# Sample attention of a hybrid decoder trunk: two batches in one softmax tile, and value products by head pair in 32-column groups

## The chip, the cores and the metric

The kernel runs on one core of a Trainium2 chip. The metric is the time of one execution on the device in microseconds (us). The core has a matrix engine (TensorE, PE in the rows; its weight loads are PEld), VectorE (DVE), ScalarE (ACT), GpSimd (POOL), SyncE (SP), which here only issues DMAs, and 16 DMA engines. PE multiplies a stationary operand of up to 128x128 with a moving one; a product with 32 stationary columns uses one of four groups of 32 columns of the array and writes the 32 partitions of PSUM that belong to it.

## The reference

Two decoder layers over one prompt of 512 tokens and 8 sample batches of 8 new tokens. Each layer has three mixers (GLA, HGRN2 and softmax attention), an output projection and a channel mixer. The change is in the softmax attention of the sample batches. It has 8 heads of 64 dims, and each new token sees 1024 cached keys and the new ones at three dilations:

```python
def dilated_attention_sample(q, k, v, kbuf, vbuf):
    kc = jnp.concatenate([kbuf.astype(k.dtype), k], axis=1)
    vc = jnp.concatenate([vbuf.astype(v.dtype), v], axis=1)
    parts = []
    for window, dil in DILATED_GROUPS:       # ((128, 1), (512, 4), (2048, 16))
        band = window // dil
        idx = buf + jnp.arange(T)[:, None] - dil * jnp.arange(band + 1)[None, :]
        valid = idx >= 0
        kg = kc[:, idx]
        vg = vc[:, idx]
        s = jnp.einsum('bthd,btkhd->bthk', q, kg).astype(jnp.float32) * scale
        s = jnp.where(valid[None, :, None, :], s, -jnp.inf)
        m = jnp.max(s, axis=-1)
        p = jnp.exp(s - m[..., None])
        parts.append((m, jnp.sum(p, axis=-1), jnp.einsum('bthk,btkhd->bthd', p, vg.astype(jnp.float32))))
    return combine_dilations(parts), kc[:, T:], vc[:, T:]
```

The kernel computes all three dilations as one softmax over all 1024 + 64 keys, with the logarithm of how often a key occurs in the three groups added to its score (`smask` for the cache, `smask_new` for the new keys, where those of other batches are masked away).

## The kernel before

Every engine has its own program, written by hand, and they meet on semaphores. A layer runs through the input projections, the linear mixers, the prompt attention, the sample attention, the output projection (L882 among others) and the channel mixer.

The sample attention (PE program L1082 to L1123) loops over 8 batches `b`. Its state:

- `Qs` holds, for each batch and head pair `hp` (0 to 3), a 128x32 stationary operand: two heads of 64 dims in rows, 8 tokens of the first head in columns 0 to 7, 8 of the second in 8 to 15. The other 16 columns are zero. VectorE writes it in L1499 and L1503, just ahead of the prompt attention.
- The scores of a batch stand in PSUM banks 0 to 2. Head pair `hp` has partitions 32hp to 32hp+31, of which 16 are live. The products are L1105 (1024 cached keys, in two of 512) and L1106 (64 new keys).
- VectorE scales and masks them into a softmax tile `Ps` in L1543 and L1545 and takes the maximum in L1548; ScalarE takes the exponential and its sum in L790; VectorE takes the reciprocal in L1557. PE transposes the tile (L1092, L1093), and ScalarE copies it out of PSUM (L785, L786) into `PTs`.
- Values: for each of 8 chunks of 128 keys, one product with the transposed tile as stationary operand (128 columns, all head pairs) and all 512 value columns as moving one (L1118), and one over the new keys (L1120). Each 32-row group thus also gets the columns of the three other head pairs, which nobody reads.
- VectorE takes the 128 columns of each head pair and scales them into `Os` (L1534, four instructions of 32 rows). PE turns `Os` (L1096), and VectorE copies both halves into `mix` (L1553, L1554), the input of the output projection.

PE runs in an interleaved order: in step `b` it transposes the tile of batch b-1, turns the output of b-2, makes the scores of b and the values of b-1.

The cache of keys and values comes in pieces of 1 MB, four a batch (keys in two pieces by head pairs, L481; values in two halves of four chunks, L484). There are 7 buffers. `piece_order` sets the order, SP issues the DMAs in it, and from the eighth piece on it first waits until PE has used the piece that had the buffer: `ssc_done` (after a batch's scores) for keys, `spv_half` and `spv_done` (after each half of a batch's values) for values. The first 7 are issued before the prompt attention.

All products of this stage are float32. The trace shows each as two passes, with a weight load each.

## Time and profile before

| | |
|---|---|
| median of 3 runs | 2908.32 us (2907.53 to 2909.29) |
| profiled execution, its span | 2910.4 us |
| PE busy | 2689.7 us, 92% |
| VectorE busy | 940.2 us, 32% |
| ScalarE busy | 637.7 us, 22% |
| GpSimd busy | 229.2 us, 8% |
| DMA | 360.60 MB, mean 124 GB/s |

The profile is of one execution, 2.1 us above the median. "Busy" is the share of time in which an instruction of the engine is recorded; passes of PE that run over each other are counted once. PEclk is the clock granted to TensorE, where 1.00 is 2.4 GHz and 0.50 is 1.2 GHz. A row of a timeline gives start, length, engine, line, operation, tiles and count, and in brackets how long the engine had sat idle and for whom. A row of a window gives its bounds and length, then busy time and count of instructions of PE, PEld, VectorE, ScalarE and GpSimd, the granted clock, the busy share of the 16 DMA engines and their GB/s. A count of passes is twice that of float32 products.

### The profile page before, as it was taken

The page shows a single profiled execution, that of the slowest core. Times are in us where ns is not written, and L with a number is a line of the kernel's source. Part 1 is how long each engine was busy: PE and PEld are TensorE (multiplying, and loading weights), DVE is VectorE, ACT ScalarE, POOL GpSimd, SP SyncE. Part 2 cuts the span into 40 slices and gives each one's busy share as a digit, 9 for nine tenths or more (in the row PEclk, how much of TensorE's full clock was granted, in tenths as well). Part 3 has the DMA queues.
Part 4 walks back from the last instruction along what each step waited for, and adds up shares of the span by engine and source line. Part 5 has one row for each costly group of instructions (what it writes and reads, how often), then busy time and mean ns, then how long its engine had stood idle before and what let it go on. Part 6 is the DMA issues. An engine that isn't in the chain of part 4 may idle for free. (4 is left out here: it accounts for less than half of the span.)

```text
span 2910.4 us, 36713 instructions
## 1 busy us (share of the span) xinstructions
PE 2689.7 (92%) x14894; PEld 2134.0 (73%) x14894; DVE 940.2 (32%) x1787; ACT 637.7 (22%) x1092; POOL 229.2 (8%) x328
## 2 busy tenths in 40 slices
PE   7996878999799999999888889998999999999998
PEld 5993444535599999979744444467899999999996
DVE  3237454322223223133465443312022222222122
ACT  3453222211222122133622232101010000000000
POOL 2003331000100000020042210000000000000000
PEclk9997565599899999999866656997799999999997
DMA  4531003073364464235200032701454644555461
GB/s 159 184 130 48 0 1 117 1 260 116 129 225 152 150 230 147 64 121 182 102 4 1 2 116 85 277 15 42 127 179 138 213 161 162 171 180 159 137 213 57
DMA packets 79894, 360.60 MB, mean 124 GB/s; under 512 B 9296, under 2 KB 9696, under 8 KB 70816
## 3 DMA queue, kind: packets, MB, share of 16 engines
q1 hardware_dynamic: 76640, 350.85, 35.5%
q0 software_dynamic: 3136, 8.06, 0.8%
q8 instruction: 88, 1.44, 0.2%
q14 instruction: 30, 0.25, 0.0%
HBM read 350.03 MB, written 75.43 MB: 146 GB/s over the span
## 5 line engine op out<-in xcount | busy, mean ns | idle before, releaser
L1258 PE MATMUL ps<-scratch,weight_ring 128*128 128x160 f32 x2816 | 398.9, 300 | 1.5 <-ACT scratch L839 1.4
L1258 PEld LDWEIGHTS ps<-scratch,weight_ring 128*128 128x128 f32 x2816 | 388.8, 191 | 2.3 <-ACT scratch L839 1.9
L888 PE MATMUL ps<-ffn_in_hi,weights_hi 128*128 128x288 f32 x704 | 210.5, 299 | 23.3 <-DVE weights_lo L1578 22.1
L1733 DVE TENSOR_TENSOR scratch<-scratch,ps 128x160 f32<-128x160 f32 x88 | 28.2, 321 | 609.2 <-ACT scratch L855 609.2
L1263 PE MATMUL ps<-scratch,weight_ring 128*128 128x160 f32 x1408 | 211.0, 304 | 0.0
L888 PE MATMUL ps<-ffn_in_lo,weights_hi 128*128 128x288 f32 x704 | 209.3, 297 | 0.0
L888 PE MATMUL ps<-ffn_in_hi,weights_lo 128*128 128x288 f32 x704 | 208.5, 296 | 0.0
L1263 PEld LDWEIGHTS ps<-scratch,weight_ring 128*128 128x128 f32 x1408 | 193.8, 190 | 10.5 <-issue 10.5
L888 PE MATMUL ps<-proj_in_hi,proj_weights_hi 128*128 128x288 f32 x608 | 182.6, 300 | 0.0
L855 ACT ACTIVATE scratch<-ps 128x160 f32<-128x160 f32 x88 | 26.8, 304 | 708.7 <-PE ps L1258 708.7
L888 PE MATMUL ps<-proj_in_lo,proj_weights_hi 128*128 128x288 f32 x608 | 179.3, 295 | 0.0
L888 PE MATMUL ps<-proj_in_hi,proj_weights_lo 128*128 128x288 f32 x608 | 178.7, 294 | 0.0
L888 PEld LDWEIGHTS ps<-ffn_in_hi,weights_hi 128*128 128x128 f32 x704 | 133.5, 190 | 24.2 <-issue 24.2
L1210 PE MATMUL ps<-scratch,values 128*128 128x160 f32 (+1 forms) x720 | 137.8, 339 | 4.3 <-DVE scratch L1673 4.3
L888 PEld LDWEIGHTS ps<-ffn_in_hi,weights_lo 128*128 128x128 f32 x704 | 134.2, 191 | 0.0
L888 PEld LDWEIGHTS ps<-ffn_in_lo,weights_hi 128*128 128x128 f32 x704 | 133.9, 190 | 0.0
L1210 PEld LDWEIGHTS ps<-scratch,values 128*128 128x128 f32 (+1 forms) x720 | 111.1, 204 | 30.0 <-issue 30.0
L882 PE MATMUL ps<-normed_or_mixed,weight_ring 128*128 128x288 f32 x512 | 128.1, 414 | 1.1 <-DVE normed_or_mixed L1554 1.1
L731 ACT ACTIVATE scratch<-scratch 128x448 f32<-128x448 f32 (+22 forms) x198 | 75.2, 390 | 213.8 <-POOL scratch L574 96.5
L882 PEld LDWEIGHTS ps<-normed_or_mixed,weight_ring 128*128 128x128 f32 x512 | 99.2, 194 | 29.4 <-DVE normed_or_mixed L1554 1.5
L1578 DVE TENSOR_TENSOR weights_lo<-weight_ring,weights_hi 128x1024 fp32r<-128x1024 f32 (+1 forms) x60 | 80.2, 1343 | 119.2 <-ACT weights_hi L806 119.2
L994 PE MATMUL ps<-scratch,constants 128*64 128x512 f32 x192 | 106.6, 674 | 10.6 <-DVE scratch L1439 7.8
(298 smaller groups left out, 4505.7 us busy)
## 6 DMA issues: line engine op xcount, KB each, us to landing
weight_ring<-w_gu SPq DMA_DIRECT2D x220, 512.0 KB, 4.2
weight_ring<-w_dn_moe SPq DMA_DIRECT2D x88, 512.0 KB, 3.6
ok_s<-kcache SPq DMA_DIRECT2D x16, 2032.0 KB, 10.2
ov_s<-vcache SPq DMA_DIRECT2D x16, 2032.0 KB, 9.9
scratch<-kcache SPq DMA_DIRECT2D x20, 1024.0 KB, 7.3
scratch<-vcache SPq DMA_DIRECT2D x20, 1024.0 KB, 5.7
weight_ring<-w_feat SPq DMA_DIRECT2D x38, 512.0 KB, 3.7
linear<-vcache SPq DMA_DIRECT2D x12, 1024.0 KB, 6.5
```

What stands on the lines that cost most here:

```text
L731: nc.scalar.activation(v, v, ACT.Exp).then_inc(exp_ready, 1)
L855: nc.scalar.activation(tg[:, f % 2, :], ps[:, 3 + f % 2, 0:CAP], ACT.Silu).then_inc(silu_ready, 1)
L882: op = nc.tensor.matmul(out_pair[:, a, :], w, rhs[:, a * HALF:a * HALF + HALF], start=k == 0, stop=k == kn - 1)
L888: op = nc.tensor.matmul(out, x, y, start=k == 0 and n == 0, stop=k == kn - 1 and n == 2)
L994: nc.tensor.matmul(ps[0:64, 0, :], const["to_row"][:, o:o + 64], Pr[:, j % 2, 0:SEQ], start=j == 0, stop=j == BLK - 1).then_inc(prod_used, 1)
L1210: op = nc.tensor.matmul(out, H_tok[0:rows, tt, k * P:k * P + P], Sel[0:rows, tt, :], start=tt == 0, stop=tt == TT)
L1258: op = nc.tensor.matmul(ps[:, 3 + f % 2, o:o + CAP], w[:, k, :], Xg[:, k, :], start=k == 0, stop=k == KC - 1)
L1263: op = nc.tensor.matmul(ps[:, k // 3, (k % 3) * CAP:(k % 3) * CAP + CAP], w[:, k, :], hidg[:, f, :], start=f == 0 and k % 3 == 0, stop=f = ...
L1578: v.tensor_tensor(Wl[:, j % NSPLIT, 0:w], ring[:, n % R, 0:w], Wh[:, j % NSPLIT, 0:w], ALU.subtract).then_inc(w_split, 1)
L1733: v.tensor_tensor(hidg[:, f, :], tg[:, f % 2, :], ps[:, 3 + f % 2, CAP:2 * CAP], ALU.mult).then_inc(hid_ready, 1)
```

## The change

Two batches share one softmax tile. The 32 stationary columns of a head pair now hold 16 of the even batch (`i` = 0) and 16 of the odd (`i` = 1); for each batch the other half of the columns is zero. The scores of both are accumulated in the same PSUM rows. The loop runs over 4 pairs `u`, so mask, maximum, exponential, transposes, copies and the turn of the output come once per pair. In the scores the head pairs are now the inner loop, ahead of the two halves of keys.

The value product of a chunk is four products per batch, one per head pair: 32 stationary columns, and as moving operand the head pair's own 128 value columns. The two batches accumulate in banks 6 and 7, each for all 32 rows of a head pair. VectorE takes the right rows of both by multiplying with two columns (`rden_pair`), the reciprocal sum in the rows of one batch and zero in the others. Both are added into `Os`. The query copies become 16 instead of 8. `piece_order` now has the keys of a pair ahead of the values of the pair before.

```diff
-CONSTS = [("ones", P), ("lnc", SEQ), ("smask", PAST), ("smask_new", NB * NS), ("cos", T), ("sin", T), ("mask16", P),
+NPAIR = NB // 2
+CONSTS = [("ones", P), ("lnc", SEQ), ("smask", PAST), ("smask_new", NPAIR * NS), ("pair_rows", 2), ("cos", T), ("sin", T), ("mask16", P),
...
     row = p % 32
     t = row % DEC
-    live = row < 2 * DEC
     d = PAST + t - np.arange(PAST)[None, :]
-    c["smask"] = np.where(live, log_mult(d, d >= 0), 0).astype(np.float32)
+    c["smask"] = log_mult(d, d >= 0)
...
+        new.append(log_mult(d, (d >= 0) & (key // DEC == 2 * pair + row // (2 * DEC))))
+    c["pair_rows"] = (row // (2 * DEC) == np.arange(2)[None]).astype(np.float32)
...
-        piece_order = [(b - (part >= 2), part) for b in range(NB + 1) for part in range(4)
-                       if 0 <= b - (part >= 2) < NB]
+        piece_order = [(2 * (u - lag) + b, 2 * lag + half) for u in range(NPAIR + 1) for lag in range(2) if 0 <= u - lag < NPAIR
+                       for b in range(2) for half in range(2)]
...
-                for b in range(NB + 2):
-                    q = (b - 1) % 2
-                    if 1 <= b <= NB:
-                        n = NB * L + b - 1
+                for u in range(NPAIR + 2):
+                    q = (u - 1) % 2
+                    if 1 <= u <= NPAIR:
+                        n = NPAIR * L + u - 1
                         pe.wait_ge(sp_ready, n + 1)
-                        if b >= 2:
+                        if u >= 2:
                             pe.wait_ge(spt_ready, n)
                         for c in range(8):
                             nc.tensor.transpose(ps[:, 3 + c // 4, (c % 4) * P:(c % 4) * P + P], Ps[:, q, c:PAST:8], const["ident"])
                         nc.tensor.transpose(ps[0:NS, 5, 0:P], Ps[:, q, PAST:PAST + NS], const["ident"]).then_inc(spt_ps, 1)
-                    if b >= 2:
-                        pe.wait_ge(os_ready, NB * L + b - 1)
-                        nc.tensor.transpose(ps[:, 6 + b % 2, 0:P], Os, const["ident"]).then_inc(os_turned, 1)
-                    if b < NB:
-                        n = NB * L + b
-                        kc = [tiles(piece_landed(pe, L, b, part), 2) for part in range(2)]
-                        if b:
-                            pe.wait_ge(ssc_free, n)
-                        for hp in range(4):
-                            o = slice(32 * hp, 32 * hp + 32)
+                    if u >= 2:
+                        pe.wait_ge(os_ready, NPAIR * L + u - 1)
+                        nc.tensor.transpose(ps[:, 6, P:2 * P], Os, const["ident"]).then_inc(os_turned, 1)
+                    if u < NPAIR:
+                        if u:
+                            pe.wait_ge(ssc_free, NPAIR * L + u)
+                        for i in range(2):
+                            b = 2 * u + i
+                            kc = [tiles(piece_landed(pe, L, b, part), 2) for part in range(2)]
                             for a in range(2):
-                                nc.tensor.matmul(ps[o, a, :], Qs[:, b, hp, :], kc[hp // 2][:, hp % 2, a * 512:a * 512 + 512], start=True, stop=True)
-                            op = nc.tensor.matmul(ps[o, 2, 0:NS], Qs[:, b, hp, :], QK[:, 4 + hp, SEQ:T], start=True, stop=True)
-                        op.then_inc(ssc_done, 1)
-                    if 1 <= b <= NB:
-                        n = NB * L + b - 1
+                                for hp in range(4):
+                                    nc.tensor.matmul(ps[32 * hp:32 * hp + 32, a, :], Qs[:, b, hp, :], kc[hp // 2][:, hp % 2, a * 512:a * 512 + 512],
+                                                     start=i == 0, stop=i == 1)
+                            for hp in range(4):
+                                op = nc.tensor.matmul(ps[32 * hp:32 * hp + 32, 2, 0:NS], Qs[:, b, hp, :], QK[:, 4 + hp, SEQ:T],
+                                                      start=i == 0, stop=i == 1)
+                            op.then_inc(ssc_done, 1)
+                    if 1 <= u <= NPAIR:
+                        n = NPAIR * L + u - 1
                         pe.wait_ge(spt_ready, n + 1)
-                        if b >= 3:
-                            pe.wait_ge(smix_ready, n - 1)
-                        pt, out = tiles(PTs[:, q, :], 9), ps[:, 6 + q, :]
-                        for half in range(2):
-                            vc = tiles(piece_landed(pe, L, b - 1, 2 + half), 4)
-                            for c in range(4):
-                                op = nc.tensor.matmul(out, pt[:, 4 * half + c, :], vc[:, c, :], start=(half, c) == (0, 0), stop=False)
-                            if half:
-                                op = nc.tensor.matmul(out, pt[0:NS, 8, :], V[0:NS, TT, 512:1024], start=False, stop=True)
-                            op.then_inc((spv_half, spv_done)[half], 1)
-                pe.wait_ge(smix_ready, NB * (L + 1))
+                        if u >= 2:
+                            pe.wait_ge(smix_ready, n)
+                        pt = tiles(PTs[:, q, :], 9)
+                        for i in range(2):
+                            b = 2 * (u - 1) + i
+                            for half in range(2):
+                                vc = tiles(piece_landed(pe, L, b, 2 + half), 4)
+                                for c in range(4):
+                                    for hp in range(4):
+                                        o = slice(32 * hp, 32 * hp + 32)
+                                        op = nc.tensor.matmul(ps[o, 6 + i, 0:P], pt[:, 4 * half + c, o], vc[:, c, hp * P:hp * P + P],
+                                                              start=(half, c) == (0, 0), stop=False)
+                                if half:
+                                    for hp in range(4):
+                                        o = slice(32 * hp, 32 * hp + 32)
+                                        op = nc.tensor.matmul(ps[o, 6 + i, 0:P], pt[0:NS, 8, o], V[0:NS, TT, 512 + hp * P:512 + hp * P + P],
+                                                              start=False, stop=True)
+                                op.then_inc((spv_half, spv_done)[half], 1)
+                pe.wait_ge(smix_ready, NPAIR * (L + 1))
...
-                        op = v.tensor_copy(Qs[r, :, hp, hb * DEC:hb * DEC + DEC], QK[r, hp, SEQ:T].rearrange("p (b t) -> p b t", b=NB))
+                        for i in range(2):
+                            o = (2 * i + hb) * DEC
+                            op = v.tensor_copy(Qs[r, i:NB:2, hp, o:o + DEC], QK[r, hp, SEQ:T].rearrange("p (b t) -> p b t", b=NB)[:, i:NB:2])
...
-                for b in range(NB + 2):
-                    if b >= 2:
-                        dve.wait_ge(spv_done, NB * L + b - 1)
-                        if b >= 3:
-                            dve.wait_ge(os_turned, NB * L + b - 2)
-                        for hp in range(4):
-                            r = slice(32 * hp, 32 * hp + 32)
-                            op = v.tensor_scalar(Os[r], ps[r, 6 + b % 2, hp * P:hp * P + P], rden[r, 4 + b % 2:5 + b % 2], None, ALU.mult)
-                        op.then_inc(os_ready, 1)
-                        dve.wait_ge(os_ready, NB * L + b - 1)
-                    if b < NB:
-                        n = NB * L + b
-                        pn, s = Ps[:, b % 2, :], 4 + b % 2
-                        dve.wait_ge(ssc_done, n + 1)
-                        if b >= 2:
+                for u in range(NPAIR + 2):
+                    pair_col = rden_pair[:, 2 * (u % 2):2 * (u % 2) + 2]
+                    if u >= 2:
+                        dve.wait_ge(spv_done, NB * L + 2 * (u - 1))
+                        link(v.tensor_scalar(Os, ps[:, 6, 0:P], pair_col[:, 0:1], None, ALU.mult))
+                        v.scalar_tensor_tensor(Os, ps[:, 7, 0:P], pair_col[:, 1:2], Os, ALU.mult, ALU.add).then_inc(os_ready, 1)
+                        dve.wait_ge(os_turned, NPAIR * L + u - 1)
+                        o = ps[:, 6, P:2 * P].rearrange("p (h i x) -> p h i x", h=4, i=2)
+                        t = SEQ + 2 * DEC * (u - 2)
+                        for hb in range(2):
+                            r = slice(hb * DH, hb * DH + DH)
+                            op = v.tensor_copy(mix[r, 4:8, t:t + 2 * DEC].rearrange("p h (i x) -> p h i x", i=2), o[r, :, :, hb * DEC:hb * DEC + DEC])
+                        op.then_inc(smix_ready, 1)
+                    if u < NPAIR:
+                        n = NPAIR * L + u
+                        pn, s = Ps[:, u % 2, :], 4 + u % 2
+                        dve.wait_ge(ssc_done, NB * L + 2 * (u + 1))
+                        if u >= 2:
                             dve.wait_ge(spt_ps, n - 1)
                         v.scalar_tensor_tensor(pn[:, 0:PAST], ps[:, 0:2, :].rearrange("p a t -> p (a t)"), DH ** -0.5,
                                                const["smask"], ALU.mult, ALU.add)
                         v.scalar_tensor_tensor(pn[:, PAST:PAST + NS], ps[:, 2, 0:NS], DH ** -0.5,
-                                               const["smask_new"][:, b * NS:b * NS + NS], ALU.mult, ALU.add).then_inc(ssc_free, 1)
+                                               const["smask_new"][:, u * NS:u * NS + NS], ALU.mult, ALU.add).then_inc(ssc_free, 1)
                         dve.wait_ge(ssc_free, n + 1)
                         v.tensor_reduce(negmax[:, s:s + 1], pn, AX.X, ALU.max, negate=True).then_inc(smx_ready, 1)
-                    if b >= 2:
-                        dve.wait_ge(os_turned, NB * L + b - 1)
-                        o = ps[:, 6 + b % 2, 0:P].rearrange("p (h q) -> p h q", h=4)
-                        t = SEQ + DEC * (b - 2)
-                        v.tensor_copy(mix[0:DH, 4:8, t:t + DEC], o[0:DH, :, 0:DEC])
-                        v.tensor_copy(mix[DH:P, 4:8, t:t + DEC], o[DH:P, :, DEC:2 * DEC]).then_inc(smix_ready, 1)
-                    if b < NB:
+                    if u < NPAIR:
                         dve.wait_ge(sp_ready, n + 1)
                         link(v.reciprocal(rden[:, s:s + 1], den[:, s:s + 1]))
+                        link(v.tensor_scalar(pair_col, const["pair_rows"], rden[:, s:s + 1], None, ALU.mult))
```

ScalarE's loop changes in the same manner, from `b` and `NB` to `u` and `NPAIR`, with the same instructions.

PE, a middle step of the loop, before. L1092 and L1093 are transposes, L1096 the turn of the output, L1105 and L1106 the scores, L1118 and L1120 the values; `linear` and `scratch` are the memories that hold buffers and tiles:

```order
L1092 MATMUL ps<-constants,scratch 128x128 x8
L1093 MATMUL ps<-constants,scratch 64x128
L1096 MATMUL ps<-constants,linear 128x128
L1105 MATMUL ps<-linear 32x512 x2
L1106 MATMUL ps<-attn_qk,linear 32x64
...
L1118 MATMUL ps<-scratch 128x512 x8
L1120 MATMUL ps<-values,scratch 128x512
```

PE, the same place now, one step for a pair (L1107 and L1110 are the scores, L1126 and L1131 the values):

```order
L1094 MATMUL ps<-constants,scratch 128x128 x8
L1095 MATMUL ps<-constants,scratch 64x128
L1098 MATMUL ps<-constants,linear 128x128
L1107 MATMUL ps<-linear 32x512 x8
L1110 MATMUL ps<-attn_qk,linear 32x64 x4
L1107 MATMUL ps<-scratch,linear 32x512 x8
L1110 MATMUL ps<-attn_qk,linear 32x64 x4
L1126 MATMUL ps<-scratch 32x128 x32
L1131 MATMUL ps<-values,scratch 32x128 x4
L1126 MATMUL ps<-linear,scratch 32x128 x32
L1131 MATMUL ps<-values,scratch 32x128 x4
```

The eight products 512 wide have become 32 products 128 wide for each batch, the scores of four head pairs follow each other, and one set of transposes serves two batches.

VectorE, a middle step before (L1534 scales the output, L1543 to L1548 prepare the softmax, L1553 and L1554 copy to `mix`):

```order
L1534 TENSOR_SCALAR linear<-ps,small 32x128 x4
L1543 SCALAR_TENSOR_TENSOR scratch<-ps,constants 128x1024
L1545 SCALAR_TENSOR_TENSOR scratch<-ps,constants 128x64
L1548 TENSOR_REDUCE small<-scratch 128x1
L1553 COPY normed_or_mixed<-ps 64x4x8
L1554 COPY normed_or_mixed<-ps 64x4x8
L1557 RECIPROCAL small<-small 128x1
```

VectorE, the output part of a step now, at the end of a layer's sample attention:

```order
L1545 TENSOR_SCALAR linear<-ps,small 128x128
L1546 SCALAR_TENSOR_TENSOR linear<-ps,small,linear 128x128
L1552 COPY normed_or_mixed<-ps 64x4x16 x2
```

Four instructions of 32 rows have become two of 128 rows, and the copies to `mix` come right behind the output's turn, ahead of the next pair's softmax.

SP, the pieces of the cache at the start of a layer's sample attention, before:

```order
L481 DMA scratch<-kcache 128x2048 x4
L484 DMA linear<-vcache 128x2048 x2
L481 DMA linear<-kcache 128x2048
L481 DMA scratch<-kcache 128x2048
L484 DMA scratch<-vcache 128x2048 x2
```

And now:

```order
L483 DMA scratch<-kcache 128x2048 x4
L483 DMA linear<-kcache 128x2048 x3
L483 DMA scratch<-kcache 128x2048
L486 DMA scratch<-vcache 128x2048 x3
L486 DMA linear<-vcache 128x2048
```

Eight pieces of keys now lead, then the four of values of the first pair.

## Rows read from the trace of the kernel before

**Rows 1.** The page: span, and busy time of each engine

```profile
span 2910.4 us, 36713 instructions
PE 2689.7 (92%) x14894; PEld 2134.0 (73%) x14894; DVE 940.2 (32%) x1787; ACT 637.7 (22%) x1092; POOL 229.2 (8%) x328
```

**Rows 2.** Busy time by window: both stages, and one steady batch

```profile
579.30:704.70 125.40, 115.91 (x417) 47.45 (x417) 36.03 (x80) 19.78 (x32) 0.00 (x0) 0.99 0.56 210
1790.80:1916.20 125.40, 115.88 (x417) 47.41 (x417) 36.03 (x80) 19.79 (x32) 0.00 (x0) 0.99 0.56 209
605.57:620.21 14.64, 14.26 (x53) 5.91 (x53) 4.48 (x10) 2.45 (x5) 0.00 (x0) 1.00 0.78 289
```

**Rows 3.** Timeline of PE, one batch

```profile
617.24 1.12 PE L1120 MATMUL ps<-values,scratch 64*128 64x512 f32 x2
618.29 1.17 PE L1092 MATMUL ps<-constants,scratch 128*128 128x128 f32 x8
...
619.95 0.33 PE L1096 MATMUL ps<-constants,linear 128*128 128x128 f32 x1 [0.38 <-DVE linear L1534]
620.21 1.93 PE L1105 MATMUL ps<-scratch,linear 128*32 128x512 f32 x6
...
624.82 7.13 PE L1118 MATMUL ps<-linear,scratch 128*128 128x512 f32 x16
```

**Rows 4.** State update in 32-column groups: timeline, all instructions of the line, window

```profile
291.21 1.08 PE L1017 MATMUL ps<-values,scratch 128*32 128x64 f32 x32 [0.51 <-DVE scratch L1469]
...
L1017 PE MATMUL ps<-values,scratch x128: 313/314/369, 291.2 to 1656.4; 128*32 128x64 f32 x64, 128*64 128x64 f32 x64
...
291.20:292.30 1.10, 1.09 (x34) 0.92 (x36) 0.00 (x0) 0.00 (x0) 0.00 (x0) 0.50 0.00 0
```

**Rows 5.** Timeline: the first softmax of layer 0

```profile
584.04 1.23 DVE L1543 SCALAR_TENSOR_TENSOR scratch<-ps,constants 128x1024 f32<-128x1024 f32 x1 [10.61 <-PE ps L1106]
...
585.43 1.28 DVE L1548 TENSOR_REDUCE small<-scratch 128x1 f32<-128x1088 f32 x1
586.75 1.20 ACT L790 ACTIVATE scratch<-scratch,small 128x1088 f32<-128x1088 f32 x1 [7.50 <-DVE small L1548]
...
588.10 1.25 PE L1092 MATMUL ps<-constants,scratch 128*128 128x128 f32 x8 [4.09 <-ACT scratch L790]
```

**Rows 6.** DMA in the stage of layer 0, and windows of it

```profile
q1 hardware_dynamic: 3600, 26.22, 56.2%
...
584.00:585.00 1.00, 0.00 (x1) 0.00 (x0) 0.96 (x1) 0.00 (x0) 0.00 (x0) 1.00 0.17 33
...
586.00:587.00 1.00, 0.00 (x0) 0.00 (x0) 0.71 (x1) 0.25 (x1) 0.00 (x0) 1.00 0.87 344
587.00:591.00 4.00, 2.90 (x11) 1.38 (x12) 0.16 (x1) 2.22 (x4) 0.00 (x0) 0.75 0.92 387
599.00:605.00 6.00, 5.91 (x20) 2.63 (x18) 1.30 (x5) 0.76 (x3) 0.00 (x0) 1.00 1.03 414
...
629.00:633.00 4.00, 4.00 (x10) 1.31 (x8) 0.16 (x1) 0.00 (x0) 0.00 (x0) 1.00 1.01 426
```

**Rows 7.** Granted clock by window (PEclk): prompt attention, after a wait, output projection

```profile
440.00:579.00 139.00, 127.07 (x398) 70.57 (x396) 55.19 (x153) 38.47 (x107) 12.46 (x20) 0.50 0.16 62
...
588.10:592.40 4.30, 4.30 (x15) 1.74 (x17) 0.14 (x1) 1.18 (x2) 0.00 (x0) 0.61 0.59 248
...
704.70:708.50 3.80, 3.80 (x9) 2.75 (x10) 0.00 (x0) 0.00 (x0) 0.00 (x0) 0.55 0.00 0
708.50:712.30 3.80, 3.80 (x17) 2.96 (x17) 0.00 (x0) 0.00 (x0) 0.00 (x0) 1.00 0.01 4
```

**Rows 8.** Timeline: the end of layer 0's sample attention

```profile
702.28 1.43 DVE L1534 TENSOR_SCALAR linear<-ps,small 32x128 f32<-32x128 f32 x4 [8.28 <-PE ps L1120]
```

**Rows 9.** Timeline: query copies and the first step of the prompt attention

```profile
470.10 1.21 DVE L1503 COPY linear<-attn_qk 64x64 f32<-64x64 f32 x8
...
471.69 1.64 PE L1059 MATMUL ps<-attn_qk 64*128 64x384 f32 x2 [0.94 <-DVE scratch L1514]
```

More of the change, by code:

```diff
@@ L268, in build @@
         rden = SM[:, 56:64]
+        rden_pair = SM[:, 0:4]
         ebl = tiles(SM[:, 64:64 + CT * 12], CT)
@@ new lines, in _ @@
+                    if 1 <= u <= NPAIR:
+                        n = NPAIR * L + u - 1
+                        pe.wait_ge(spt_ready, n + 1)
+                        if u >= 2:
[16 more added lines that the diff above has]
+                                op.then_inc((spv_half, spv_done)[half], 1)
```

18 lines of the change are left out of this document (8 added, 10 removed).

## The prediction

> **What bounds the kernel now.** I read the page first: one core, span 2910.4 us, TensorE busy 92%, VectorE 32% [rows 1]. Such an average does not say what the edited stage is worth, so the second view is busy time by window. The sample attention runs once in each layer, 579.3 to 704.7 and 1790.8 to 1916.2 us: twice 125.4 us, with PE busy 115.9 of them and DMA at a share of 0.56 [rows 2]. A window of one steady batch lasts 14.64 us, PE busy 14.26 in it; VectorE has 4.5 us of work, ScalarE 2.5 [rows 2]. So eight batches in a row are bound by PE, and the next resource is the DMA (0.78 of its time), not the softmax.
>
> The third view is PE's order in time. A float32 product appears in the trace as two passes. In a batch the value products take 7.13 us for their 16 passes of 512 columns, 0.45 us each, and the one over the new keys 1.12 more; from the first transpose to the turn of the output pass 1.66 us, 0.38 of it a wait, so the transposes take 1.3, and the turn 0.33 [rows 3]. What is left of the batch, from 620.21 to 624.82, is 4.6 us of scores [rows 3]. Summed serially, 16 score passes at 0.45 us would be 7.2 us: passes of different 32-column groups already run over each other, though the order (all of one head pair, then the next) lets only neighbours do so.
>
> **PE's part of the change.** The value product of a chunk is now four products of 128 columns, each in its own 32-column group, instead of one of 512. Per batch that is 36 products, 72 passes, for 9 products, 18 passes. The cost hangs on whether four groups run together. The state update shows exactly this pattern, four heads in four 32-column groups, one after another: 32 passes end 1.08 us after the first begins, 34 ns apiece, where one pass alone is recorded with at least 313 ns, at a granted clock of 0.50 (1.2 GHz) [rows 4]. Four passes together are 135 ns for 64 columns at half clock, so 135 ns for 128 columns at full clock if the rate follows the clock. From the other side, a 512-column pass of 0.45 us gives 0.11 us for 128 columns. 18 sets a batch are therefore 2.0 to 2.4 us; I take 2.2, against 8.2 now.
>
> The scores get head pairs innermost, so four groups follow each other directly: 4 passes of 0.45 plus two short ones, 1.9 us a batch. The other bound is no more overlap than now, 4.6 us. I take 1.9, nearest to the update's row; no row shows four groups at full clock, so 4.6 stays in the range. Transposes (1.3), the output turn (0.33) and their waits come once per pair.
>
> At full clock PE then needs for a pair of batches 3.8 (scores) + 4.4 (values) + 1.3 + 0.3 + about 0.5 of waits = 10.3 us, 15.7 with the scores' upper bound. Before, it was 2 x 14.64 = 29.3.
>
> **The softmax chain.** From VectorE's start to the first transpose, 584.04 to 588.10, pass 4.1 us: 1.23 and 1.28 on VectorE and 1.20 on ScalarE are most of it [rows 5]. With PE's step ahead of it I count 4.2. The tiles keep their size but serve two batches; rows that were dead are used, and time goes by columns. So the chain occurs four times a layer instead of eight, and beside it lie the value products of the previous pair (4.4 us). Only the first is exposed, as before; the DMA bound below covers it. PE waits twice more for an output to be copied out, both once per pair, behind transposes.
>
> **What becomes late: the cache.** None of this changes the bytes. 25 pieces of 1 MB are loaded inside a stage (7 sit there when it starts), 26.22 MB on the hardware queue [rows 6]. Where the queue is full, the lowest and the highest of five windows of 4 to 6 us show 414 and 426 GB/s, at shares of 1.03 and 1.01 [rows 6]. At 420 GB/s a piece is 2.5 us, a pair of batches (8 pieces) 20.0 us. That is nearly double PE's 10.3: the stage turns from PE-bound to DMA-bound, and most of PE's gain is lost. With 7 buffers, a DMA needs only the buffer seven pieces back. In pair rhythm PE's longest stretch without a release (transposes, turn, first scores) is about 4 us, less than two pieces' time, so the queue should stay full once it is.
>
> The stage per layer by steps:
> - first batch's scores until its buffers come free: 1.9 us;
> - issue to flowing data: 1.5 us (33 GB/s in the first microsecond, 344 in the third [rows 6]);
> - a gap while PE waits for the first softmax and then scores batch 2. PE is back at 3.8 + 4.2 + 1.3 = 9.3 us, ends batch 2 at about 11 to 12.5 (the clock has been 0.5 after this wait [rows 7]), and four pieces have been queued until then: they land until 3.4 + 10 = 13.4. The next data flow at 12.5 to 14. I take 0.7;
> - 26.22 MB at 420 GB/s: 62.4 us;
> - the last half batch of values, 10 sets of passes, 1.1 us at full clock to 2.7 at half: 1.6;
> - the tail. Now 2.4 us, from 702.28 to the stage's end at 704.7, of it 1.43 for four copies of 32 rows [rows 2, 8]; afterwards two of 128 rows at 0.35 each: 1.9 with the wait ahead.
>
> Sum 70.0 us, against 125.4: 55.4 saved.
>
> **What it costs elsewhere.** The query copies on VectorE are 16 instead of 8, each half as long. 8 take 1.21 us, and VectorE's first step of the prompt attention comes behind them, for which PE then waits 0.94 us [rows 9]. Between 0 and 1.2 us are added; 0.8 taken. A stage in which PE waits half the time may hand a low clock to the output projection: there 3.80 us at 0.55 did 9 passes, and the next 3.80 at 1.00 did 17 [rows 7], so each 3.8 us more at half clock costs 1.8. Part of this is paid already; 1.0 taken, 0 to 2. The constants shrink by 254 columns, at nothing: they load at the start, behind other work. Two layers: 2 x (55.4 - 1.8) = 107.2; 2910.4 - 107.2 = 2803.2 us. The median of the runs, 2908.32, is 2.1 below the profiled span, so I forecast **2801 us**.
>
> **The clock.** The rows show PE at 0.61 right after a 4 us wait, and at 0.50 through the whole prompt attention though PE was called busy 127 of 139 us [rows 7]. So in a stage that waits for data 1.2 GHz is possible throughout. Then values are 8.8, scores 7.6, transposes and turn 3.4: 19.8 us a pair by my upper value price, about 18 by the lower, still at or under 20.0.
>
> The Trainium skill (TensorE: Matmul & The Clock Gate, "HAM oscillation") says that a loop whose compute bursts are shorter than its DMA waits is put back to half clock in each burst. By that rule this stage runs at 1.2 GHz, which makes the first rival below the outcome; the rows just named agree that it falls after a wait, and none shows a DMA-paced stage.
>
> **Rivals.** (1) *Turns instead of cover.* At 1.2 GHz PE has no slack, and the 3.4 us at the head of each pair, in which no buffer is released, add to the 20.0 instead of lying beside them: 4 x 3.4 x 2 = 27 us, 2828 us. For it: the clock rows. Against: seven buffers. (2) *A slower stream.* No row shows more than some 8 us of full queue without a pause; the new stage asks for over 60. At 387 GB/s, a window in which the queue filled [rows 6], it is 67.8 us instead of 62.4: 2812 us. (3) *Slower than before.* The small products don't overlap: 72 passes a batch at 0.11 us are 7.9, scores in series 7.2 a batch, a pair 15.8 + 14.4 + 2.1 = 32.3 us against 29.3, so 12 us a layer: 24 more than 2908, 2932 us. It decides from 29.3 us a pair, that is once both products lose nearly all overlap. Against it stand the rows of the update, and the scores of today that already overlap.
>
> **How the numbers follow.** DMA-bound with little lost, 2790 to 2812: 0.71. Rival 2, 2812 to 2822: 0.08. Rival 1 or a part of it, 2822 to 2840: 0.13. Rival 3: 0.04. The rest, 0.04, lies between 2840 and 2900. The low end is 426 GB/s (1.8 us less), no cost for copies and clock (3.6), no gap (1.4) and a last half batch at full clock (1.0): 2793, rounded down. Range 2790 to 2840, which leaves out less than 1 in 10 by these cases; I keep it there since no case ends between. Measurement tells 0.2% (6 us) from no change. Faster 0.95, same 0.01, slower 0.04.
>
> **What would show each step.** In the profile after: the stage near 70 us in both layers; DMA share near 1.0 and about 400 GB/s over it; PE busy clearly under its length if the clock is high; value passes starting four together, about 27 to 34 ns apiece. PE's waits should be for pieces that land, not for VectorE or ScalarE. Wrong if DMA pauses at each pair's head (rival 1), if its share is full at fewer GB/s (rival 2), or if value passes start 0.1 us apart (rival 3). The output projection's first 4 us tell the clock term.

## The result

The changed kernel takes 2805.94 us, median of 4 runs (2803.39 to 2809.07), against 2908.81 of the kernel before (4 runs): a ratio of 0.9647, interval 0.9633 to 0.9661. The forecast was 2801. A second series of 5 runs gave 2808.24, ratio 0.9655 (0.9641 to 0.9669). The profiled execution lasted 2803.6 us; the sum of the prediction was 2803.2.

The page after, which answers to [rows 1]:

```profile
span 2803.6 us, 38139 instructions
PE 2544.7 (91%) x15678; PEld 2087.7 (74%) x15678; DVE 902.4 (32%) x1715; ACT 617.5 (22%) x1060; POOL 230.5 (8%) x328
```

PE is still called busy 91% of the span. What happened is seen by window only: first both stages, then four stretches of them (us, busy time and instructions of PE, PEld, DVE, ACT and POOL, granted clock, DMA share, GB/s). They answer to [rows 2] and [rows 6].

```profile
575.90:648.10 72.20, 47.02 (x809) 27.44 (x809) 16.71 (x36) 9.89 (x16) 0.00 (x0) 0.91 0.90 365
1732.00:1808.00 76.00, 48.49 (x815) 27.72 (x813) 16.71 (x36) 10.49 (x17) 0.00 (x0) 0.88 0.86 346
592.00:600.00 8.00, 4.47 (x109) 3.20 (x98) 2.93 (x8) 2.47 (x4) 0.00 (x0) 1.00 1.01 423
600.00:610.00 10.00, 6.75 (x88) 2.74 (x91) 1.27 (x2) 0.00 (x0) 0.00 (x0) 0.83 1.01 424
630.00:640.00 10.00, 6.26 (x158) 4.62 (x159) 2.74 (x7) 2.47 (x4) 0.00 (x0) 1.00 1.02 420
1760.00:1770.00 10.00, 8.75 (x84) 3.32 (x88) 1.06 (x1) 0.00 (x0) 0.00 (x0) 0.55 1.01 424
```

From the first score product to the output projection it is now 72.1 us in layer 0 (575.94 to 648.08) and 74.6 in layer 1 (1733.35 to 1807.99), against 125.3 twice. PE works 47 of 72 us. In the four short windows DMA stands at a share of 1.01 or 1.02 and 420 to 424 GB/s, both where PE was busy 56% and where it was busy 88%, mostly at half clock (0.55). This looks as if the bound had moved to the cache's transfer; the first experiment tests it.

PE's timeline shows what became cheap (start, duration, engine, line, tile, count, in brackets the wait ahead and what ended it); it answers to [rows 3] and [rows 5]:

```profile
575.94 1.92 PE L1107 MATMUL ps<-scratch,linear 128*32 128x512 f32 x16 [0.73 <-issue]
583.92 1.59 PE L1094 MATMUL ps<-constants,scratch 128*128 128x128 f32 x8 [4.12 <-ACT scratch L792]
590.43 1.92 PE L1126 MATMUL ps<-scratch 128*32 128x128 f32 x64
592.28 0.42 PE L1131 MATMUL ps<-values,scratch 64*32 64x128 f32 x8
592.63 1.08 PE L1126 MATMUL ps<-scratch 128*32 128x128 f32 x32
599.98 1.92 PE L1107 MATMUL ps<-linear 128*32 128x512 f32 x16 [2.94 <-DMA linear<-kcache]
604.97 3.59 PE L1107 MATMUL ps<-scratch,linear 128*32 128x512 f32 x16 [2.95 <-DMA scratch<-kcache]
625.00 3.27 PE L1107 MATMUL ps<-scratch,linear 128*32 128x512 f32 x16 [2.93 <-DMA scratch<-kcache]
642.44 1.08 PE L1126 MATMUL ps<-scratch 128*32 128x128 f32 x32 [1.06 <-DMA scratch<-vcache]
644.90 1.08 PE L1126 MATMUL ps<-scratch 128*32 128x128 f32 x32 [1.38 <-DMA scratch<-vcache]
647.20 0.33 PE L1098 MATMUL ps<-constants,linear 128*128 128x128 f32 x1 [0.86 <-DVE linear L1546]
```

A batch's values are 64 passes in 1.92 us, 30 ns apiece, and with the new keys 2.2 us from 590.43 to 592.63. From 594.30 on most stretches of scores or values start behind a piece that lands.

The trace's DMA records give each piece's landing. Each piece leaves 16 records, one for each DMA engine's part, and counts when the last is there. The records do not name the engine: "first engine" stands for a piece's earliest record, "slowest" for its latest. Worked out from them, in us (the third column is for the last piece):

```
                 queue's   stream of the   landing of   last landing   from there to
                 start     first engine:   slowest      from stage's   the output
                 latency   gaps in it      behind first start          projection
layer 0          1.8       0.98            1.95         68.92          3.22
layer 1          1.8       1.24            4.03         71.27          3.37
```

The first column is the time from SP's first issue, 2.1 us into the stage, to the first engine's first landing, less a piece's 2.485 us. Twenty-five pieces at 2.485 us (422 GB/s) are 62.1. In layer 0 that is 2.1 + 1.8 + 62.1 + 0.98 + 1.95 = 68.9.

### The profile page after: what moved, and what is told of

Read it like the earlier page. It is cut to its first block, busy times and chain, and to the rows that moved or that the text cites. A ratio compares the mean times of both kernels' runs of the same rounds, so it can differ in the third digit from the quotient of the medians.

```text
span 2803.6 us, 38139 instructions
## 1 busy us (share of the span) xinstructions
PE 2544.7 (91%) x15678; PEld 2087.7 (74%) x15678; DVE 902.4 (32%) x1715; ACT 617.5 (22%) x1060; POOL 230.5 (8%) x328
## 4 chain that ended last, share of the span: by engine, by line
PE 84%; DVE 6%; DMA 4%; ACT 3%; issue 2%; POOL 1%; SPq 0%; DVEq 0%; ACTq 0%; POOLq 0%
PE ps L890 24%; PE ps L1270 14%; PE ps L1275 7%; PE ps L884 7%; PE ps L1222 5%; PE ps L1244 4%; PE ps L931 4%; PE ps L1061 3%; PE ps L1080 2%; DMA scratch<-kcache 2%; PE ps L996 2%; PE ps L988 2%; PE ps L1069 1%; PE ps L1035 1%; DVE scratch L1451 1%
```

## The experiments

Two theories stood against each other for most of them. *DMA*: the stage is paced by the landings, and PE and the softmax lie under them. *PE or softmax*: a remaining wait between engines paces it. A second question was which of the change's parts brings the gain: the values by groups, the head pairs innermost in the scores, or the pairing. "Stage" is as above, layer 0 and layer 1 of the profiled execution.

### Half the bytes

```diff
+                            w = 1 if at < NPC else 2
-                                sp.dma_start(tiles(pieces[slot], 2), d["kcache"][L, b][:, 2 * part:2 * part + 2]).then_inc(piece_in[slot], 16)
+                                sp.dma_start(tiles(pieces[slot], 2)[:, :, 0:1024 // w], d["kcache"][L, b][:, 2 * part:2 * part + 2, 0:1024 // w]).then_inc(piece_in[slot], 16)
```

`w` is 2 from the eighth piece on, so half of the cache is left out. The values' pieces are halved in the same way.

> The changed kernel, but from the eighth piece of a layer on only half of each cache piece is loaded (half of the keys' columns, two of four value chunks); the products run over all columns as before, on old data. So half of the cache is left out, and the work of every engine is unchanged. My theory (the stage is paced by the DMA): the data take 31 us instead of 62, PE becomes the bound with about 10.3 us a pair, and the stage falls from 72 to 74 us to 47 to 52 us in each layer. Rival (turns instead of cover, PE at 1.2 GHz with some 19 us a pair): the stage stays near 65 to 70 us. Rival (PE or the softmax chain paces the stage already): it stays at 72 or more.

The stages took 52.0 and 50.5 us, 20.1 and 24.2 less. The total, 2862.4 us in one run, can't be compared: the stage's wrong values go on to the later parts, and PE does 16366 passes instead of 15678. In the stage nothing was left out but bytes:

```profile
592.00:612.00 20.00, 17.01 (x332) 10.84 (x332) 6.84 (x16) 4.95 (x8) 0.00 (x0) 1.00 1.02 380
```

The *DMA* theory holds: with the same instructions on PE, VectorE and ScalarE the stage shrinks by 20 us or more. It doesn't show a stage that is free of the DMA, though. PE fills 85% of these 20 us, and the DMA share is still 1.02, at 380 GB/s: halving a piece also changed its packets, 4752 for 13.11 MB in layer 0 where the changed kernel has 3600 for 26.22. The stage came out in the upper part of the expected 47 to 52 us.

### The groups one after another

```diff
-                                for c in range(4):
-                                    for hp in range(4):
+                                for hp in range(4):
+                                    for c in range(4):
```

> The changed kernel, with the head pairs as the outer loop of the value products: the 16 passes of one 32-column group (8 at a time, per half batch) come before those of the next, with the same products. Theory (what makes 72 passes a batch cheap is that four groups run together, which needs neighbours in the order): the passes of one group follow each other at 0.107 us, and only neighbours at the seams overlap, as in the old scores. A batch's values then take 4 to 7.5 us instead of 1.9 to 2.2, a pair of batches 14 to 21 us of PE. Below 20 us the DMA still hides it and the stage stays at 72 to 76 us; above, it grows by 4 times the excess, at most to 85. Rival (the array keeps all four groups busy whatever the order): value passes still start 27 ns apart.

Ratio 0.9662 (0.9644 to 0.9680), stages 76.0 and 77.1 us, about at the upper end of what was expected. PE's timeline, one batch at full clock:

```profile
612.89 4.34 PE L1126 MATMUL ps<-scratch 128*32 128x128 f32 x64
617.16 0.42 PE L1131 MATMUL ps<-values,scratch 64*32 64x128 f32 x8
```

The same 64 passes take 4.34 us instead of 1.92 when eight passes, four products, in a row go to the same group. That more than doubles the price of the values. In layer 0's stage PE is busy 62.8 us instead of 47.0, and yet the stage is only 3.8 us longer (2.5 in layer 1), and the ratios, 0.9662 and 0.9655 for the changed kernel, are not told apart; their intervals are too wide to show these 6 us. In layer 0 the last piece lands 69.4 us after the start (68.9 without the edit), and most of the extra appears behind it, 6.5 us to the projection instead of 3.2, where nothing covers PE's work. In layer 1 it lands at 72.2 (71.3), and the projection starts 5.0 us later (3.4). The overlap of four groups is real, but inside the stage most of it isn't needed.

### Pairs with wide values

The tiles of pairs stay; L1126 and L1131 become one product of 128x512 and one of 64x512 per chunk again, and VectorE scales in eight steps of 32 rows.

> The changed kernel with the pair tile, but each batch's value products as before: 128 stationary columns and 512 value columns for each chunk, and VectorE takes the blocks it needs (eight instructions of 32 rows). It has the pairing and the new score order, without the 32-column groups for values. PE needs 3.8 + 16.4 + 1.6 + 0.5 = 22.3 us a pair, over the DMA's 20.0. Theory: stage 4 x 22.3 plus about 8 for the first scores, the first softmax and the end = 97 us, 28 below the kernel before, about 2853 us in all. If pairing were worthless, it would be 104 or more (the score order alone).

Ratio 0.9829 (0.9806 to 0.9853), stages 104.9 and 105.0: slower than expected by 8 us, and inside the range that the expectation gave for pairing that is worth nothing. The timeline shows one reason:

```profile
609.86 1.12 PE L1126 MATMUL ps<-values,scratch 64*128 64x512 f32 x2
610.91 1.16 PE L1094 MATMUL ps<-constants,scratch 128*128 128x128 f32 x8
611.91 0.27 PE L1095 MATMUL ps<-constants,scratch 128*64 128x128 f32 x1
614.04 0.33 PE L1098 MATMUL ps<-constants,linear 128*128 128x128 f32 x1 [1.86 <-DVE linear L1545]
```

The eight scalings stand between the last value product and the turn, and PE waits about 1.86 us for them in each pair (3.00 behind the last). A pair takes 23.4 us (614.04 to 637.47), bound by PE. Pairing and the order of the scores together bring 48 us in the medians (2910.6 to 2862.4) without the groups, under half of the gain. How little of it is the pairing's shows below, where the order stands alone.

### Groups for the values, no pairs

```diff
-                                op = nc.tensor.matmul(out, pt[:, 4 * half + c, :], vc[:, c, :], start=(half, c) == (0, 0), stop=False)
+                                for hp in range(4):
+                                    o = slice(32 * hp, 32 * hp + 32)
+                                    op = nc.tensor.matmul(out[o, 0:P], pt[:, 4 * half + c, o], vc[:, c, hp * P:hp * P + P], start=(half, c) == (0, 0), stop=False)
...
-                        for hp in range(4):
-                            r = slice(32 * hp, 32 * hp + 32)
-                            op = v.tensor_scalar(Os[r], ps[r, 6 + b % 2, hp * P:hp * P + P], rden[r, 4 + b % 2:5 + b % 2], None, ALU.mult)
+                        v.tensor_scalar(Os, ps[:, 6 + b % 2, 0:P], rden[:, 4 + b % 2:5 + b % 2], None, ALU.mult).then_inc(os_ready, 1)
```

The base is the kernel before; scores and softmax remain per batch.

> The kernel before, one batch per tile and its old score order, with only the value products by head pair in 32-column groups, and one scaling instruction of 128 rows instead of four. PE per batch: 4.6 scores + 2.0 values + 1.6 transposes and turn = 8.2 us, plus what shows of the softmax chain: 4.2 us from the last score to the next transposes, of which the values cover only 2.0, so about 2 us more, and 0.4 of wait for the turn. 10.8 us a batch against 10.0 of the DMA. Theory: stage 8 x 10.8 + 6 = 92 us, 33 below the kernel before, about 2842 us. If the softmax chain is hidden, the stage is DMA-bound at 84 to 87 as 8 x 10 plus ends.

Ratio 0.9730 (0.9714 to 0.9746), median 2831.2; stages 89.2 and 89.1, 3 us under the expected 92. Two rows of PE's timeline, a batch apart, and a window:

```profile
605.49 1.16 PE L1092 MATMUL ps<-constants,scratch 128*128 128x128 f32 x8 [2.05 <-ACT scratch L790]
...
615.63 1.16 PE L1092 MATMUL ps<-constants,scratch 128*128 128x128 f32 x8 [2.05 <-ACT scratch L790]
```

```profile
605.00:625.00 20.00, 16.18 (x212) 9.06 (x212) 6.88 (x14) 4.67 (x9) 0.00 (x0) 1.00 0.99 391
```

A batch is 10.14 us, 2.05 of it a wait for the exponential. The DMA moves 391 GB/s, close to the 422 of the changed kernel but not there.

### The order of the scores alone

Base is the kernel before; the head pairs become the inner loop in the scores, the values stay 512 wide.

> The kernel before with one edit: in the scores the head pairs are innermost, so four 32-column groups follow each other. One batch per tile, value products 512 columns wide. Scores fall from 4.6 to 1.9 us a batch; nothing waits newly, since the 8.2 us of value products cover the softmax. Theory: a batch takes 14.64 - 2.7 = 11.9 us, the stage 8 x 2.7 = 21 to 22 us less than 125.3, that is 104 us, about 2864 to 2868 us in all. Since the run with the pair tile and wide values had 105 us, pairing without narrow values would then have been worth nothing. Rival (pairing is worth what it saves on transposes): this stage is 110 us or more.

Ratio 0.9850 (0.9835 to 0.9865), stages 105.0 and 104.2.

```profile
606.96 0.62 PE L1105 MATMUL ps<-scratch,linear 128*32 128x512 f32 x2
606.97 0.62 PE L1105 MATMUL ps<-linear 128*32 128x512 f32 x2
...
608.70 0.29 PE L1108 MATMUL ps<-attn_qk,linear 128*32 128x64 f32 x8
608.93 6.28 PE L1120 MATMUL ps<-linear,scratch 128*128 128x512 f32 x14
```

The scores of a batch last 2.0 us, 606.96 to the first value pass at 608.93, instead of 4.6 [rows 3]: 2.6 us for each of 8 batches, 21 a stage. The stage is 1 us over the expected 104 or on it, the median, 2863.6, just under the expected range. With pairs on top, two sections above, the stage was the same 105 us: as long as the values stay wide, pairing brought nothing. Two batches take 24.0 us here and 23.4 as a pair, and that is lost again at the end: in layer 0 two batches of values instead of one stand behind the last softmax, and a wait of 3.00 us for the scalings instead of 1.52.

### Both orders, no pairs

The two edits above together.

> The kernel before with one batch per softmax tile, but both of PE's regroupings: value products by head pair in 32-column groups, and head pairs innermost in the scores. Per batch PE does 1.9 + 2.2 + 1.6 us and waits about 2 to 2.5 for the softmax, whose 4.2 us are covered only by the values: 7.7 to 8.2 us a batch, under the DMA's 10.0. Theory (the DMA is the bound and pairing only makes PE's share smaller below it): stage 71 to 76 us, like the changed kernel, some 2800 to 2812 us in all. Rival (pairing is what brings the stage below 89 us): 85 us or more, 2825 and up.

Ratio 0.9653 (0.9636 to 0.9669), median 2808.10: the same as the changed kernel's 2808.24 beside it. In steady state the DMA is full too:

```profile
605.00:625.00 20.00, 13.18 (x224) 7.73 (x216) 6.88 (x14) 5.08 (x9) 0.00 (x0) 0.93 1.01 422
```

The stages are 77.6 and 77.4, above the expected range. SP's issues and the landings say why. Timeline of SP:

```profile
580.34 0.33 SPq L481 DMA_DIRECT2D scratch<-kcache  x1
580.72 8.92 SPq L484 DMA_DIRECT2D scratch<-vcache  x2
589.68 0.43 SPq L481 DMA_DIRECT2D scratch<-kcache  x1
```

Before the first softmax only one batch's keys can be released, so two pieces are queued (580.34, 580.72), and the queue then runs dry: 4.4 us of gap in the first engine's stream. Pairs release four pieces there, and the gap is 1.0. This is the larger part of what pairing does for the stage, 5 us per layer in the profile: 3.4 and 3.3 us are the gap, 1.1 and 0.9 a slowest engine that is further behind (3.05 and 3.25 us against 1.98 and 2.32), 0.8 and 0.6 the way from the last landing to the projection. In the total it isn't seen. In this profile the parts around the stage, which the edit doesn't touch, were shorter by 5.1 us in all than in the changed kernel's beside it (span 2806.0 less 155.0 against 2800.8 less 144.7); whether that is chance or has a cause is left open.

### The scores of the second pair first

In the changed kernel the first softmax leaves PE idle for 4.12 us. Here the scores of pair 1 are issued ahead of the transposes of pair 0, in that wait.

`scores()` is the block of score products, unchanged, put in a function.

```diff
+                    if u == 1:
+                        scores()
                     if 1 <= u <= NPAIR:
...
+                    if u != 1:
+                        scores()
```

> The changed kernel with one move on PE: the scores of the second pair come ahead of the transposes of the first, so they fill the 4 us in which PE waits for the first softmax, and the buffers of the second pair's keys come free some 5 us earlier. Theory (the stage lost time in the gap before the twelfth piece, whose buffer waits for batch 2's scores): the landings stay 2.48 us apart from the first to the last, no gap of 3.5 or 4.5 us between the fourth and fifth, the last piece lands 1 to 3 us earlier after the stage's start, stage 69 to 72 us, 2 to 6 us less in all than the changed kernel. Rival (the gap is start-up latency of the queue or one lagging DMA engine, whatever the order): the landings keep their gap and nothing moves.

> The changed kernel itself, as a reference for the next two on the same chip. Expected 0.9647 of the kernel before, as measured (0.9633 to 0.9661), stages of 72 to 75 us.

Ratio 0.9637 (0.9618 to 0.9655) beside 0.9655 (0.9641 to 0.9669) for the changed kernel: the intervals overlap. Stages 71.1 and 72.1 against 72.2 and 72.5. The landings separate two things. The gap in the first engine's stream fell from 1.03 to 0.08 us in layer 0 and from 1.05 to 0.77 in layer 1. The slowest engine's delay did not: 1.98 and 2.32 us before, 1.73 and 2.26 now. So the theory was half right: in layer 0 PE's late release makes the gap of one microsecond. In layer 1 it makes about half of it: 0.5 of the 1.05 us stood between the fourth and the sixth landing and is gone, and 0.5 stood between the first and the second, where no release is late; that time is 3.00 us without the edit and 3.21 with it. The three later traces with this order have 0.0 to 0.3 us of gap in both layers.

### Work for PE's waits

PE waits 18 us of layer 0's stage and 20 of layer 1's for the DMA. The first four of the output projection's eight k-steps read only what the linear mixers left, and so need nothing of the sample attention. In this kernel, on top of the last edit, the first four k-steps of its units 0 and 1 are issued between the last value pieces.

```diff
+EARLY_OUT = {(3, 0, 1): 0, (4, 0, 0): 1}
...
+                                m = EARLY_OUT.get((u, i, half))
+                                if m is not None:
+                                    pe.wait_ge(ssc_free, NPAIR * (L + 1))
+                                    w = landed(ring_n + m)[:, 0:1024].rearrange("p (k c) -> p k c", k=KC)
+                                    for k in range(4):
+                                        gemm(pair(m), w[:, k, :], mix[:, k, :], k, KC)
...
-                    for k in range(KC):
+                    for k in range(4 if m in EARLY_OUT.values() else 0, KC):
```

> The kernel of the run before last (second pair's scores first), and in PE's waits for the last cache pieces the first half (four of eight steps, the ones that read the linear mixers' outputs) of the first two units of the output projection: 32 passes, 7.7 us of work for each layer, moved from behind the stage into it. Theory (PE is idle for 5 us or more of each 10 us there, and only the DMA paces the stage): the stage does not get longer by more than 1 us, the projection behind it is 7.7 us shorter, 13 to 16 us less in all than the run before last. Rival (PE at 1.2 GHz has no time to give): the stage grows by as much as the projection shrinks, and the gain is under 5 us.

> The kernel with the early first halves of two units of the output projection, again, as the reference of the run before it on the same chip: 0.9587 of the kernel before (0.9572 to 0.9602), stage 74 us in both layers.

2789.29 us, ratio 0.9587 (0.9572 to 0.9602), and again 2787.74, 0.9586 (0.9573 to 0.9599). It is 14 us below the kernel of the last section, as expected, and 0.7% below the changed kernel. PE's timeline at the end of layer 0's stage:

```profile
629.66 4.15 PE L885 MATMUL ps<-normed_or_mixed,weight_ring 128*128 128x288 f32 x16
...
639.52 4.15 PE L885 MATMUL ps<-normed_or_mixed,weight_ring 128*128 128x288 f32 x16
643.60 1.08 PE L1132 MATMUL ps<-scratch 128*32 128x128 f32 x32
644.61 0.42 PE L1137 MATMUL ps<-values,scratch 64*32 64x128 f32 x8
644.96 1.95 PE L1132 MATMUL ps<-scratch 128*32 128x128 f32 x64
```

8.3 us of projection were moved, and the stage grew from 71.1 to 73.8: 5.6 us hidden; in layer 1, 72.1 to 73.8, it is 6.6. That the stage would grow by no more than 1 us was wrong. The last 64 value passes have no wait ahead of them, since the last piece had landed at 643.2. More than that: from 629.66 on PE doesn't wait for a piece any more (its only wait up to the last values is 1.16 us for ScalarE, ahead of 638.51). PE has become the bound of the last 20 us.

### More of it

The last four k-steps over the first 288 tokens, which are all prompt tokens, are moved too, for both units: 4.4 us more.

> As the early projection, with more of it: of the first two units also the last four steps over the first 288 tokens, which are all prompt tokens, so 24 of 32 passes of each unit, 5.8 us twice in each layer, now stand in PE's waits for the last eight value pieces. PE is idle there some 11 us. Theory: the stage grows by 1 to 2 us against the early projection (73.8), the projection behind it shrinks by 3.9, a gain of 3 to 6 us in all. Rival (PE's slack there is used up, since each value piece already waits for a lump of 4 us): the stage grows by 3.9 or more and nothing is gained.

2785.93 us, ratio 0.9583 (0.9569 to 0.9597), not to be told from the 2787.74 beside it, so the expected gain isn't there. The trace agrees:

```profile
646.36 2.21 PE L1146 MATMUL ps<-normed_or_mixed,weight_ring 128*128 128x288 f32 x8
648.50 1.96 PE L1132 MATMUL ps<-scratch 128*32 128x128 f32 x64
```

The last piece lands at 642.3, 68.1 us after the start as before the edit. One of the two added lumps stands behind it (646.36), the other ahead of it (633.88), but in the stretch in which PE had no wait for a piece left. So neither is hidden: the stage is 78.3 us, less 12.7 moved is 65.6; before, 73.8 less 8.3 is 65.5.

## Why the prediction was right

- **What it turns on.** That the stage changes from PE-bound to DMA-bound was shown by halving the bytes and, from the other side, by doubling the price of the values: 15.8 us more of PE's work lengthened layer 0's stage by 3.8.
- **Value products**, 2.2 us a batch taken: 2.20 measured. Scores 1.9 taken: 16 passes in 1.92 at full clock. The state update's passes at half clock [rows 4] were the right row, and the rate follows the clock (34 ns for 64 columns there, 30 for 128 here).
- **26.22 MB**, 62.4 us taken: 62.1, at 422 GB/s over more than 60 us. Rival 2 (a slower stream in the long run) is out. The Trainium skill (DMA: Bandwidth & Descriptors, Bandwidth) gives 425 GB/s for a 16 MB load by a core that streams alone. The trace agrees with its 422; with the 79.0 us that the same row gives for those 16 MB, half that rate, it does not.
- **Head and tail.** First scores 2.1 (1.9 taken), start of the queue 1.8 (1.5), from the last landing to the projection 3.2 and 3.4 (1.6 + 1.9).
- **The gap** is the term that was mis-sized: 0.7 taken. It is 1.0 and 1.2 in the stream itself, and a second part wasn't in the sum at all, 2.0 and 4.0 us by which the slowest of the 16 engines lags behind the first. Together 2.9 and 5.3. So the stages are 72.1 and 74.6 instead of 70.0. Nor is all of the gap where the prediction put it, behind the first softmax: in layer 0 it is, in layer 1 0.8 of its 1.24 us stand between the first three landings.
- **Copies.** 0.8 taken; PE now waits 1.59 for the prompt attention's first step, 0.94 before [rows 9]: 0.65.

```profile
466.83 1.87 DVE L1517 COPY linear<-attn_qk 64x32 f32<-64x32 f32 x16
469.07 1.65 PE L1061 MATMUL ps<-attn_qk 64*128 64x384 f32 x2 [1.59 <-DVE scratch L1528]
```

- **The clock behind the stage.** 1.0 taken a layer. Windows of the output projection after, as [rows 7]:

```profile
648.10:651.90 3.80, 3.80 (x16) 3.02 (x17) 0.00 (x0) 0.00 (x0) 0.00 (x0) 1.00 0.00 0
1808.00:1811.80 3.80, 3.80 (x8) 2.80 (x9) 0.00 (x0) 0.00 (x0) 0.00 (x0) 0.50 0.02 4
```

In layer 0 it starts at full clock, where before it started at 0.55: 7 more passes, about 1.6 us gained. In layer 1 it starts at 0.50, and in the first 7.6 us it does 22 passes, 26 before: 0.9 us lost. Over both the term came out at no cost, where 2.0 us were priced.

- **The total.** The stages gave back 53.2 and 50.7 us, 103.8 instead of 110.8. The total still came out near, as the rest of the kernel, priced at a cost of 3.6 us, became 3.0 shorter. In it are differences that the prediction has no term for: the phases in between, by the first PE instruction of each, are shorter by 2.5 us in layer 0's linear mixer and 1.0 in layer 1's, whose code isn't touched. In layer 0 the granted clock was at its full level there for some microseconds in which it had been at half. So the closeness of 2803.6 to 2803.2 is partly luck; the sizes that stand are those of the stages. What moved the clock in the mixers was not tested.
- **Rival 1** occurred in pieces. The clock fell to half in four short stretches of layer 0, and for some 10 us at once in layer 1 (0.55 in the window 1760 to 1770 above). The scores then take 3.59 us instead of 1.92 (604.97), and the DMA still moves 424 GB/s: the seven buffers cover it, as far as these windows show (no run had fewer), which was the reason given against it. The rule of the Trainium skill (TensorE: Matmul & The Clock Gate, "HAM oscillation") that such a loop is put back to half clock in every burst is borne out for some bursts only: behind waits of 2.9 us for a piece the scores ran at full clock at 599.98 (1.92 us) and at half or near it at 604.97 (3.59) and 625.00 (3.27). The mean over the stages was still 0.91 and 0.88.
- **Rival 3**, groups that don't overlap, is out by the 30 ns.
- What the prediction did not see is that the same total can be had without pairs. It priced the change as a whole; pricing each part alone would have shown two cheap edits that already reach the DMA's bound.

## What to carry to other kernels

When an edit makes one engine's work in a stage twice as fast, price the next resource first: here the bytes and the GB/s of a full queue gave 62.4 us, 62.1 were measured, and with the terms for both ends the stage came out within 3 and 6%. PE's further speed counted little except behind the last piece. Then add what the stream costs at both ends, since latency, gaps and the slowest DMA engine are paid once per stage; of the three only the gaps answered to an edit here. And when the bound has moved to DMA, the engine that now waits has room: 8 us of later work a layer, moved into its waits, gave 14 us in the medians, more than the further reordering of the stage's own work (5, not clear of noise), until its last wait for a piece was used up.

## What was not expected of the hardware

- The slowest engine's part of a piece, once it had fallen behind, stayed behind in this kernel's trace as long as the queue was full. It lands 0.9 to 1.1 us behind the first for the first three or four pieces of the two layers. In layer 1 it jumps at two pieces and then stays, to 0.04 us, for all 19 that follow. Landings of some pieces, from the DMA records of the changed kernel:

```
layer 1   first engine   slowest engine   behind
          1747.97        1748.86          0.89
          1750.63        1753.39          2.75
          1753.38        1757.43          4.04
          1755.86        1759.92          4.07
          ...
          1800.59        1804.62          4.03
```

  What delays it is not settled. Six packets of instruction fetch, 16 KB and about 1 us each, run on the same engines in each stage, and part of the delay agrees with them in time. In layer 0 the slowest landing goes from 0.89 to 1.91 us behind at the piece beside the packet of 589.52, falls back after the gap, and goes from 1.04 to 1.69 at the first piece behind the packet of 596.41. In layer 1 the step from 2.75 to 4.04 has one beside it (1753.69), but the first and larger one, from 0.89 to 2.75, has none. No experiment took the packets away.
- The order of passes within the groups matters by a factor of 2.3: 1.92 us for 64 passes that go round four 32-column groups, 4.34 for the same 64 with eight passes (four products) in a row in one group, both at full clock.
